# A two-layer DeltaNet, RWKV-7 and retention step on one core: state reads moved, retention's products in turns, unread products added

## What is computed

```python
def step(s, xs):                       # gated DeltaNet, chunks of 64 tokens, 6 heads x 64
    u0_n, kcd_n, qk_n, qd_n, kd_n, gl_n = xs
    u = u0_n - jnp.einsum('bhcd,bhde->bhce', kcd_n, s)
    o = jnp.einsum('bhcd,bhde->bhce', qd_n, s) + jnp.einsum('bhij,bhje->bhie', qk_n, u)
    s = s * gl_n[..., None, None] + jnp.einsum('bhcd,bhce->bhde', kd_n, u)
    return s, o
...
def step(s, xs):                       # RWKV-7, token by token, 6 heads x 64
    r_t, w_t, k_t, v_t, a_t, b_t = xs
    sa = jnp.einsum('bhvk,bhk->bhv', s, a_t)
    s = s * w_t[:, :, None, :] + sa[..., None] * b_t[:, :, None, :] + v_t[..., None] * k_t[:, :, None, :]
    return s, jnp.einsum('bhvk,bhk->bhv', s, r_t)
...
def step(rs, xs):                      # retention, 4 heads, keys 32, values 64
    qd_n, kv_n = xs
    return rs * g_chunk + kv_n, jnp.einsum('bhcd,bhde->bhce', qd_n, rs)
...
x = x + jnp.concatenate([o_dn, o_rw, o_rt], axis=-1) @ W['w_out'][l]
h = _rmsnorm(x, W['ln_ffn'][l])
x = x + (_swiglu(...) if l % 2 == 0 else _moe(...))   # _moe: the top 2 of 8 experts
```

## Time and profile before

| | |
|---|---|
| median of 3 runs | 1875.71 us (1871.48 to 1880.37) |
| the profiled execution | 1875.41 us, span of its instructions 1873.6 us |
| TensorE busy | 1822.5 us (97%) |
| VectorE, ScalarE, GpSimd busy | 468.3, 249.3, 90.6 us |
| mean granted TensorE clock | 0.972 |
| layer 0 and layer 1 up to the experts | about 0 to 612 and 612 to 982 us |

### The profile page before, as it was taken

One profiled execution on the slowest core, in us unless ns is written; L12 is line 12 of the kernel. 1 busy time (PEld: TensorE's weight loads), 2 busy tenths in 40 slices (PEclk: granted clock), 3 DMA queues, 4 the chain that ended last, 5 costly groups with the idle time before them and its releaser, 6 DMA issues.

```text
span 1873.6 us, 38688 instructions
## 1 busy us (share of the span) xinstructions
PE 1822.5 (97%) x17826; PEld 995.2 (53%) x17826; DVE 468.3 (25%) x1039; ACT 249.3 (13%) x570; POOL 90.6 (5%) x118
## 2 busy tenths in 40 slices
PE   8999899999999999989999999999999999999997
PEld 6778876666666777877572333333333333333332
DVE  2436644300000343565541001000100100110031
ACT  2342222100000234222210000000000000000001
POOL 0000012100000000001210000000000000000000
PEclk9999887999999999999789999999999999999999
DMA  7330012723330433002189999999999999999992
GB/s 244 102 105 3 3 66 65 301 89 135 135 135 13 130 101 105 3 3 66 65 341 383 396 403 419 406 418 418 401 421 403 413 409 419 416 403 419 417 412 99
DMA packets 66664, 453.64 MB, mean 242 GB/s; under 512 B 10208, under 2 KB 37152, under 8 KB 42048
## 3 DMA queue, kind: packets, MB, share of 16 engines
q1 hardware_dynamic: 60704, 431.43, 57.6%
q0 software_dynamic: 5376, 19.49, 2.8%
q10 hardware_dynamic: 416, 0.16, 0.0%
HBM read 441.47 MB, written 9.60 MB: 241 GB/s over the span
## 4 chain that ended last, share of the span: by engine, by line
PE 93%; DVE 5%; ACT 1%; issue 1%; DMA 0%; DVEq 0%; SPq 0%; ACTq 0%
PE bank L541 91%; DVE ring L1408 1%; PE bank L552 1%; DVE work L1408 1%; DVE hT L1408 1%; DMA X<-x_in_dram 0%; DVE X L1408 0%; DVE work L1411 0%; DVE AV L1743 0%; ACT ring L2350 0%; DVE hT L1835 0%; DVE hT L1811 0%; ACT work L2374 0%; ACT L2263 0%; ACT L2353 0%
## 5 line engine op out<-in xcount | busy, mean ns | idle before, releaser
L541 PE MATMUL bank<-ring,hT 128*32 128x512 f32 (+2 forms) x6336 | 625.1, 537 | 0.0
L541 PEld LDWEIGHTS bank<-ring,hT 128*32 128x32 f32 (+1 forms) x6336 | 223.2, 112 | 399.7 <-issue 387.6
L541 PE MATMUL bank<-hT,ring 128*128 128x288 f32 x1632 | 404.2, 407 | 1.6 <-DVEq L1461 1.5
L541 PE MATMUL bank<-ring,work 128*32 128x512 f32 (+4 forms) x3168 | 390.8, 569 | 0.0
L541 PEld LDWEIGHTS bank<-hT,ring 128*128 128x128 f32 x1632 | 308.4, 190 | 98.0 <-issue 13.8
L1408 DVE TENSOR_TENSOR work<-work,bank 128x384 f32<-128x384 f32 (+2 forms) x142 | 77.9, 560 | 763.7 <-ACT work L2495 502.1
L541 PEld LDWEIGHTS bank<-ring,work 128*32 128x32 f32 (+3 forms) x3168 | 129.5, 116 | 238.4 <-issue 235.3
L2495 ACT ACTIVATE work<-bank 128x512 f32<-128x512 f32 (+1 forms) x48 | 26.1, 544 | 549.3 <-PE bank L541 549.3
L541 PE MATMUL bank<-ring 64*64 64x64 f32 (+11 forms) x1152 | 80.7, 286 | 5.9 <-DVE SS L1408 2.7
L541 PEld LDWEIGHTS bank<-ring 64*64 64x64 f32 (+6 forms) x1152 | 56.7, 147 | 21.2 <-issue 14.2
L2259 ACT ACTIVATE ring<-bank 128x32 f32<-128x32 f32 (+7 forms) x144 | 41.4, 335 | 196.9 <-PE bank L541 172.9
(11 more groups left out here) (257 smaller groups left out, 1061.9 us busy)
## 6 DMA issues: line engine op xcount, KB each, us to landing
ring<-moe_dram SPq DMA_DIRECT2D x168, 2048.0 KB, 11.1
ring<-ffn_dram SPq DMA_DIRECT2D x22, 1536.0 KB, 13.1
ring<-w_in_dram SPq DMA_DIRECT2D x18, 1536.0 KB, 6.6
ring<-w_out_dram SPq DMA_DIRECT2D x2, 1536.0 KB, 6.9
work<-w_out_dram SPq DMA_DIRECT2D x2, 1280.0 KB, 9.6
ring<-w_out_dram SPq DMA_DIRECT2D x2, 1280.0 KB, 10.0
ring<-w_in_dram SPq DMA_DIRECT2D x2, 1152.0 KB, 5.3
C<-consts_dram SPq DMA_DIRECT2D x1, 1912.5 KB, 16.2
```

The lines of the kernel that those rows point to most:

```text
L541: return nc.tensor.matmul(out, lhsT, rhs, start=start, stop=stop, skip_group_check=True)
```

## The change

1. `sample_chunks` loses its state reads. They become `sample_reads(l, y, part)`, 24 products each, for four decode sequences. For DeltaNet they run as `before_u` of chunks 2 and 3, for RWKV ahead of chunk 3's wait for U, one in front of each of retention's two means. ScalarE copies each half apart (`USO_ok` counts four per layer); SUT waits for the second.
2. `rt_outputs` and `rt_crossed` take the pairs of heads in turns: 0, 0, 1, 1.
3. Unread products are added: three ahead of the first level's wait for DeltaNet, six and three at inverse level 3, two ahead of RWKV's sample inputs and one behind their XV, two, one and one ahead of the U waits of DeltaNet's chunks 1 to 3, three and two ahead of the sample tile's U.
4. Between routing and the experts, the token numbers are broadcast to 32 columns, and three unread products go between the lists of the first round.
5. Each layer starts its turn of banks anew, at bank l.

```diff
         def fill(pe, *key):
 
-            b, turn = len(fills) % 8, len(fills) // 8
+            b = next_bank[0] % 8
+            turn = len([1 for v in fills.values() if v[0] == b])
+            next_bank[0] += 1
...
@@ first_level
                 b, full = fill(pe, l, y, "L0", t)
+                if y == 0 and t == 0:
+                    for _ in range(3):
+                        mm(pe, b[:, 0:P], ident, cst("ones64"))
                 wait(pe, first_T, l, 3 * y + t)
@@ inverses
                     tiles = [t for t in range(3) if lev < LEVELS[t]]
+                    if lev == 3:
+                        beats(pe, 3 if y else 6)
@@ chunk_inputs
+                if y and t == 2:
+                    beats(pe, 2)
                 freed(pe, l, y, "XT", t, LEVELS[t] - 1)
...
                 if y:
+                    beats(pe, t // 2)
                     freed(pe, l, "XV", t)
@@ chunk_outputs
                     before_u()
+                    if not y:
+                        beats(pe, (0, 2, 1, 1)[c])
                     wait(pe, U_ok, l, y * 4 + c - 1)
@@ TensorE
-            def sample_chunks(l, y, beside=lambda: None):
+            def sample_reads(l, y, part):
                 freed(pe, l, y, "W", 4)
                 wait(pe, ss_in, l, y)
-                b, full = fill(pe, l, y, "SU")
-                for q in range(NB):
+                b, full = fill(pe, l, y, "SU", part)
+                for q in range(4 * part, 4 * part + 4):
...
+            def sample_chunks(l, y, beside=lambda: None):
                 beside()
-                wait(pe, USO_ok, l, y)
+                wait(pe, USO_ok, l, 2 * y + 1)
...
+                beats(pe, 3 - y)
                 wait(pe, U_ok, l, y * 4 + 3)
@@ slot_lists
-                            i = mm(pe, wide[:, :, e], hot[0:n, t, e, :], token_ids[0:n, t:t + 1].to_broadcast([n, 64]),
+                            i = mm(pe, wide[:, 0:32, e], hot[0:n, t, e, :], token_ids[0:n, t:t + 1].to_broadcast([n, 32]),
                                    start=t == 0, stop=t == 2)
+                        if r == 0 and e in (2, 4, 6):
+                            mm(pe, banks[5][:, 0:P], ident, cst("ones64"))
@@ TensorE's order
+                next_bank[0] = l
...
-                chunk_outputs(l, 0, 2)
+                chunk_outputs(l, 0, 2, lambda: sample_reads(l, 0, 0))
                 rw_products(l, 1)
                 chunk_reads(l, 0, 3)
-                chunk_outputs(l, 0, 3)
+                chunk_outputs(l, 0, 3, lambda: sample_reads(l, 0, 1))
...
                 def outputs_and_cross():
-                    rt_outputs(l)
-                    rt_crossed(l)
+                    rt_outputs(l, (0,))
+                    rt_crossed(l, (0,))
+                    rt_outputs(l, (1,))
+                    rt_crossed(l, (1,))
...
                 def rt_means():
+                    sample_reads(l, 1, 0)
                     wait(pe, rtO_ok, l, 1)
-                    means(l, RT_KS)
+                    means(l, RT_KS[:1])
+                    sample_reads(l, 1, 1)
+                    means(l, RT_KS[1:])
@@ ScalarE
-            def sample_chunks(l, y):
-                b, free = take(act, l, y, "SU")
-                copy(USO[:, :, :, :].rearrange("p a b c -> p (a b c)"), b[:, 0:192]).then_inc(USO_ok.sem, 1)
-                wait(act, USO_ok, l, y)
+            def sample_reads(l, y, part):
+                b, free = take(act, l, y, "SU", part)
+                own_cols = slice(16 * part, 16 * part + 16)
+                copy(USO[:, :, :, own_cols], b[:, 0:192].rearrange("p (a b c) -> p a b c", a=3, b=2)[:, :, :, own_cols]).then_inc(USO_ok.sem, 1)
+                wait(act, USO_ok, l, 2 * y + part)
                 nc.scalar.nop().then_inc(free, 1)
```

More of the change, by code:

```diff
@@ L437, in trunk @@
         S_ok = sig("state_ready", 8)
-        USO_ok = sig("sample_state_read", 2)
+        USO_ok = sig("sample_state_half_read", 4)
         spread_seq = ctx.enter_context(nc.semaphore("spread_steps"))
@@ L513, in trunk @@
         fills = {}
+        next_bank = [0]
         def fill(pe, *key):
-            b, turn = len(fills) % 8, len(fills) // 8
+            b = next_bank[0] % 8
+            turn = len([1 for v in fills.values() if v[0] == b])
+            next_bank[0] += 1
             assert key not in fills, key
@@ L543, in beats @@
         def beats(pe, n):
[L545 to L548, removed]
+            b = next_bank[0] % 8
+            turn = len([1 for v in fills.values() if v[0] == b])
+            if n:
+                if turn:
+                    pe.wait_ge(bank_free[b], turn)
+                for _ in range(n):
+                    mm(pe, banks[b][:, 0:P], ident, cst("ones64"))
         def tr(pe, out, in_):
@@ L1006, in _, with rt_outputs @@
             rt_key = lambda t, h: sg[:, t, 32 * h:32 * h + 32]
-            def rt_outputs(l):
+            def rt_outputs(l, pairs):
                 wait(pe, rtR_ok, l, 7)
@@ L1011, in rt_outputs @@
                 rs = keys.rearrange("p a b c -> p (a b c)")
-                for p in range(2):
+                for p in pairs:
                     b, full = fill(pe, l, "rto", p)
@@ L1021, in rt_outputs, with rt_crossed @@
                     i.then_inc(full, 1)
-            def rt_crossed(l):
+            def rt_crossed(l, pairs):
                 wait(pe, rt_state_in, l, 0)
-                for p in range(2):
+                for p in pairs:
                     b, full = fill(pe, l, "rtc", p)
@@ L2566, in _ @@
                 chunk_inputs(l, 0, 2)
+                sample_reads(l, 0, 0)
                 prompt_chunk(l, 0, 2)
+                sample_reads(l, 0, 1)
                 prompt_chunk(l, 0, 3)
@@ L2570, in _ @@
                 rw_decays(l, 2)
-                sample_chunks(l, 0)
                 inverses(l, 1)
@@ L2583, in _ @@
                 prompt_chunk(l, 1, 2)
+                sample_reads(l, 1, 0)
+                sample_reads(l, 1, 1)
                 prompt_chunk(l, 1, 3)
-                sample_chunks(l, 1)
                 head_roots(l, RT_KS, GROUP_EPS)
```

## The result

The changed kernel takes **1882.0 us** (median of seven runs, 1880.74 to 1893.97) against 1871.39 us for the kernel before on the same chip: **1.0063 times, 95% interval 1.0045 to 1.0081**. It is slower by 0.63% where I had forecast 0.9% faster.

What follows compares the result with a forecast made beforehand. It took TensorE to bound the kernel, with time to gain only at its waits in the mixers or at half clock. Terms summed to -16.4 us from 1875.4, giving 1859.0 us, range 1851 to 1867.

Steps and rivals of the forecast that it cites:

- +0.1 + 1.4 + 1.4 + 2.4: Added us: unread products at first level and chunk 1; DeltaNet's halved reads; RWKV's sample inputs; RWKV's reads ahead of chunk 3.
- RWKV's reads, +2.4 us: RWKV's state reads moved ahead of chunk 3's U wait: partly hidden, but uncovering VectorE's squares, net 1.2 us slower per layer.
- DeltaNet's halves, +1.4 us: DeltaNet's chunks 2 and 3: a half plus one unread product overruns each U wait, 0.7 us slower per layer.
- The clock over this stretch: RWKV's tail through retention: short clock falls go, a last 14 us one stays, saving 11.5 us in layer 0, 4.1 in layer 1.
- Zero by itself: Retention's products in turns: same products, thin ones cut in two by full ones, costing nothing by themselves.
- I expect the short falls to go: RWKV's tail through retention: full-array products behind or between thin ones remove short clock falls, leaving 899 to 913 us.
- the -1.4 us at level 3: Inverse level 3: unread products fill the gap ahead of the fall at 786, removing 3.4 us at half clock, 1.4 us saved.
- DeltaNet's end, -2.7 us: Layer 0, end of DeltaNet: reads were last at half clock, so moving them away gains 2.7 us, otherwise about 1 us.
- rival D: DeltaNet's chunks 2 and 3: halved reads thin the stream, the clock falls at chunk 2 in both layers, 1891.5 us; chance 0.05.
- Slot lists, -2.0 us: Between routing and experts: 32 columns for 64 make each list record about 0.11 us, saving 2.0 us, bounds 0 and 4.4.
- the bounds that I gave for the tail and the lists: Tail's clock: from nothing to -17.4 us in layer 0 and -10.0 in layer 1; slot lists: 0 to -4.4 us.
- B: Whole kernel: the clock does as before and only added work counts, +4.3 us, 1879.7 us; chance 0.15.

Runs made afterwards that it cites:

- shared base: Kernel before plus only the banks' turn starting anew per layer and ScalarE copying the state reads in two halves: 1876.64 us, 1.0018 times the kernel before.
- DeltaNet's reads back: The change with DeltaNet's two halves of the state reads put back behind chunk 3, its unread products kept: 1882.91 us, 1.0055 times the kernel before.
- unread products in gaps: Kernel before plus unread products only at inverse level 3, ahead of the U waits and of the sample tile's U: 1878.89 us, 1.0030 times the kernel before.

## Why the prediction was wrong

*The work on the path was priced about right in the sum.* I had +0.1 + 1.4 + 1.4 + 2.4, 5.3 us; the change does 6.5 us more at full clock. The halves overrun, as I said (4.46 to 4.80 us from U to U at chunk 3 in layer 1). RWKV's reads, +2.4 us, measured 2.0 us. DeltaNet's halves, +1.4 us together with the unread product beside each, measured 3.1 us by themselves. What I missed is that 3.3 us come from reads and unread products together (against the shared base reads alone 1.8, unread products alone 1.6, the whole change 6.7; lists and turns nothing): they fill one wait twice.

*The step that failed is "The clock over this stretch", -11.5 and -4.1 us.* It needed 27.4 us less at half clock in layer 0's tail and 9.8 us in layer 1's, 37 us in all. The profile has 11 us less and 0.5 us more, and over the runs the whole kernel has 6 us more at half clock: some 43 us short. Two things stood behind the term, and the runs weigh them apart.

The first was full products among the thin ones. With everything but the turns the change has 92.5 us at half clock, 9 us under the kernel before; unread products alone take off 8 us (15 against the shared base). So the direction is borne out, at about a quarter of what I booked. This is the larger part of the miss, some 28 us of half clock, and why so little of it came is open.

The second was retention's products in turns, "Zero by itself". They cost 3.6 us alone and 6.8 us in the change, 10 and 15 us of half clock. I had looked at how long a thin stretch was, and not at what the cut does to the one stretch of full products. That breaking it keeps the clock down fits layer 1 of the profile of the turns alone; layer 0 of that profile, and two profiles with unbroken groups at half clock, speak against it as the rule. That the turns raise the half clock is shown; how they do it is not.

*I took falls in one trace for fixed features of the kernel.* "I expect the short falls to go": the one at 786 is missing in the change, but also where its whole wait was left; the one at 267 is gone in layer 0, and its like in layer 1 (878 before, 880.9 now) is not. So the -1.4 us at level 3 has no run behind it: alone it changes nothing in the time. In layer 0 the profiled change reached retention 5.5 us later than the kernel before (250.07 to 255.57 for the same instruction) and chunk 3's state products only 1.4 us later (286.06 to 287.44); the runs show that the first gain did not last, not what takes it.

*DeltaNet's end, -2.7 us,* rested on reads being last at half clock in layer 0. That stretch is 0.8 us longer in the profile. The clock falls at 201.8, inside the 8-column reads of chunk 2, as rival D has it, but it does so without them as well (DeltaNet's reads back). Behind it VectorE waits for ScalarE with or without the reads, as layer 1 shows at full clock.

*Slot lists, -2.0 us:* nothing to see. A narrow record takes 0.13 us, not 0.11, so the time hardly goes by the moving columns. The Trainium skill's rate for loading (TensorE: Matmul & The Clock Gate, LDWEIGHTS) gave an estimate of 0.107 us, and the row has 0.130.

*The range* of 1851 to 1867 does not come from the bounds that I gave for the tail and the lists: these reach from 1844.8 to 1876.6 us. The measured time lies outside both.

*Of the signs named,* these were right: 1.00 from 780 to 820, no fall behind the 88 records in layer 0, over 3 us ahead of DeltaNet's sample output. Others came out wrong: a fall behind the 88 records in layer 1, tails of 43.3 and 40.4 us where both were to be under 38 (over 42 in layer 0 was named as a sign of error), half clock inside DeltaNet's chunks, 7.6 us for the 42 list records where I had under 5. The nearest rival is B (clock as before, 1879.7 us), to which I gave 0.15. No load appears in the chain.

## What to carry to other kernels

Price work put into a wait by what is left of the wait after everything else that is put there, and ask what then waits behind it: here the chain went on through ScalarE, so DeltaNet's reads taken off the end gave nothing in layer 1, and fills and reads together cost 6.5 us of work. Where the clock moves from one execution to the next, don't book a gain at a single fall, and don't compare two profiles: those of one and the same kernel have one group of products at 4.12 and 6.37 us. Look first whether the fall is still there in a kernel that leaves its wait alone. Then take span and clock of a dozen runs apart into half clock and work at full clock; in the work this told parts of 2 us from each other here, where ratios could not. Moving products so that thin and full ones alternate was no free change: it cost 0.2 to 0.4% with not one instruction more.

## What the runs showed of the hardware

- The order alone of the same products changed the mean time at half clock from 108.5 to 119.0 us (turns alone against its base, standard error of the difference 4 us) and from 92.5 to 107.6 us in the change (3 us).
- The clock fell at 201.8, within 47 records of 8 columns that began at 200.67, with no wait of TensorE in the 4 us ahead (window below). The Trainium skill (TensorE: Matmul & The Clock Gate, HAM oscillation) puts such falls down to idle gaps between groups of products; this trace disagrees, as at 267 before. And a gap need not bring a fall: 1.63 us of waiting at 785.62 were followed by 4 us at 1.00 in the kernel with banks and split copy only, and by a fall in the kernel before.
- One kernel's executions can differ by more than all of these kernels' medians: 1866.29 to 1889.95 us with unread products in gaps, but 1866.27 to 1876.18 us over 24 executions with all of them. What sets the spread of a kernel is open.

Timeline and window of the change ahead of that fall:

```profile
200.67 1.79 PE L544 MATMUL bank<-ring,SS 64*64 64x8 f32 x47
...
197.80:201.80 4.00, 4.00 (x98) 3.70 (x96) 3.80 (x10) 2.37 (x6) 0.00 (x0) 1.00 0.03 6
```
